# Weight slots skewed by 64 bytes each in a two-block transformer kernel, with the delta columns moved into a spent mask

## The chip, the cores and the metric

One NeuronCore of a Trainium2 chip runs the whole kernel. The metric is the device time in microseconds (us) of one execution: the median of three runs.

## The reference

Two transformer-like blocks follow each other on a sequence of 512 tokens with 1024 channels, all in float32. The first projects its input to queries, keys, values and gates, runs a matrix LSTM over chunks and a sparse attention, and merges both. The second has a feed-forward layer (hidden width 2816), a mixer with a gated delta rule and a pooling branch, and a second feed-forward layer. Nearly all the arithmetic is in products of activations with weights:

```python
h = modulate(rms_norm(x, norm_g[l, 0]), shift[:, 0], scale[:, 0])
x = x + 0.5 * gate[:, 0, None, :] * swiglu(h, ffn1_w_in[l], ffn1_w_out[l])
h = modulate(rms_norm(x, norm_g[l, 1]), shift[:, 1], scale[:, 1])
x = x + gate[:, 1, None, :] * token_mixer(h, mix_w_in[l], conv_w[l], ...)
```

## The kernel before

**Three matmuls for one.** A float32 product is made of three matmuls in the type F32R. Each operand is split into a high part (itself, rounded to F32R) and a low part (the rest). `mm3` (lines 432 to 436) issues high weight by high activation, high weight by low activation, and low weight by high activation, all into one PSUM bank. The weight block of 128 x 128 is the stationary operand, loaded before each of the three (LDWEIGHTS, the engine PEld of the profile); the activations, 512 tokens wide, are the moving operand. Only `v1` and `vsw1` (lines 988 to 990) have the two the other way round.

**Chunks and slots.** All weights pass through four slots in turn. SyncE loads a chunk of 128 x 1024 numbers into `w_raw` (`load_chunk`, line 399); ScalarE makes the high part (`split_hi`, line 385) and VectorE the low one (`split_lo`, line 393); TensorE uses the chunk as eight blocks of 128 columns (`pe_tile`) and marks it done, which lets ScalarE write the slot again. Chunk n has slot n % 4. The splits run two chunks ahead of TensorE (`AHEAD = 2`). The list `STAGES` sets the order of chunks: `v1`, `conv1`, `small1`, `nsa1` and so on to `ffn2_out`, 307 in all. `ffn1_in` and `ffn2_in` have 44 chunks each, with `act_hi` and `act_lo` as moving operand; `ffn1_out` and `ffn2_out` have 24 chunks of 8, 8 and 6 blocks with `ffn_hi` and `ffn_lo`. Each merge takes gates from `act`, one branch from `ya` (first block) or `pool` (second), the other from `yb`; the output projections take `merged`. In the stages between `vsw1` and `merge1`, and from `k2` to `z2`, other small matmuls in plain F32 are laid between blocks of the weight chunks by hand; `mods` puts sums for the modulation between chunks in the first stages (line 894).

**The layout.** Every buffer has a fixed byte offset in its partition's row. `fixed` (line 172) places buffers one after the other from byte 16512 on, each rounded up to 32 bytes; what follows the last of them, PH, is where `phase` places buffers that share memory over time, at a given number of KB from PH:

```python
XT = fixed("residual", [KD, T])
HHI, HLO = fixed("act_hi", [KD, T], F32R), fixed("act_lo", [KD, T], F32R)
RAW = fixed("w_raw", [4, 1024])
WHI, WLO = fixed("w_hi", [4, 1024], F32R), fixed("w_lo", [4, 1024], F32R)
CST = fixed("constants", [K_ALL])
PAR = fixed("params", [PAR_ALL])
```

`residual`, `act_hi`, `act_lo`, `w_raw`, `w_hi` and `w_lo` have 16384 bytes each; `constants` has 1729 columns (6944 bytes with rounding) and `params` 984 (3936 bytes). A row ends at byte 229344. The moving operands `ffn`, `merged`, `ya`, `yb` and `pool` are phase buffers; those of `act` are fixed ones.

**The delta columns.** `delta_cols` holds nine groups of 32 columns of small per-token factors of the delta rule (`dcol`, line 508). They are written from the stage `k2` on (line 2061 and lines 2759 to 2799) and read by VectorE, ScalarE and GpSimd, and by TensorE at lines 1342 and 1343. The causal mask, 512 columns of the constants from K_CM on, is read at line 2582 in the first block's attention.

Of the kernel before, what the change touches and what calls it, by code (L numbers as in the profile page):

```python
# [19 lines left out]
F32R = mybir.dt.float32r  # L20
# [32 lines left out]
K_ID, K_ONE, K_CM, K_CMT, K_ROPE, K_SWAP, K_LV = 0, 128, 256, 768, 896, 1024, 1152  # L53
# [104 lines left out]
def two_blocks(nc, cst, x, positions, norm_g, w_in, conv_q_w, conv_q_b, conv_k_w, conv_k_b, b_igate,  # L158
# [6 lines left out]
    with ctx:  # L165
# [6 lines left out]
        def fixed(name, shape, dt=F32):  # L172
            t = nc.alloc_sbuf_tensor_at(name, [P, *shape], dt, offset=at[0])
            at[0] += -(-int(np.prod(shape)) * 4 // 32) * 32
            return t
# [1 line left out]
        XT = fixed("residual", [KD, T])  # L177
        HHI, HLO = fixed("act_hi", [KD, T], F32R), fixed("act_lo", [KD, T], F32R)
        RAW = fixed("w_raw", [4, 1024])
        WHI, WLO = fixed("w_hi", [4, 1024], F32R), fixed("w_lo", [4, 1024], F32R)  # L180
        CST = fixed("constants", [K_ALL])
        PAR = fixed("params", [PAR_ALL])
        PH = at[0]
# [1 line left out]
        def phase(name, kb, shape, dt=F32):  # L185

            off = PH + int(kb * KB)
            assert off + int(np.prod(shape)) * 4 <= 229344, (name, off, shape)
            return nc.alloc_sbuf_tensor_at(name, [P, *shape], dt, offset=off)
# [61 lines left out]
        SS, KDT = phase("delta_state", 88, [DH, P]), phase("delta_k_dec", 92, [DH, P])  # L251
        SMR2 = phase("beta_rows", 92, [T])
        ML = phase("delta_level", 96, [DH, P])
        DC = phase("delta_cols", 100, [288])
        Y2HI, Y2LO = phase("yb2_hi", 48, [KD, T], F32R), phase("yb2_lo", 64, [KD, T], F32R)
        PLHI, PLLO = phase("pool_hi", 80, [4, T], F32R), phase("pool_lo", 40, [4, T], F32R)
        PLW = phase("pool_w", 88, [4, P])
# [14 lines left out]
        def sem(name):  # L272
            if name not in names:
                names[name] = ctx.enter_context(nc.semaphore(name))
            return names[name]

        w_loaded = [sem(f"w_loaded{k}") for k in range(4)]
        w_hi, w_lo, chunk_done = sem("w_hi_ready"), sem("w_lo_ready"), sem("chunk_done")
# [229 lines left out]
        def dcol(n, k=32):  # L508
            return DC[:, n:n + k]

# [2511 lines left out]
```

## Time and profile before

| | |
|---|---|
| device time, three runs | 1966.59, 1968.11, 1969.8 us |
| median | 1968.11 us |
| profiled execution, its span | 1970.5 us |
| mean granted TensorE clock | 0.995 |
| TensorE busy, weight loads busy | 98%, 81% |
| VectorE, ScalarE, GpSimd busy | 51%, 37%, 10% |
| data moved | 212.89 MB, mean 108 GB/s |

The span is that of the profiled execution, from its first instruction to its last; the profile gives no time around it. Engines are named PE (matmuls), PEld (weight loads), DVE (VectorE), ACT (ScalarE), POOL (GpSimd) and SP (SyncE). A matmul's duration is longer than the distance to the next one's start, since they overlap in the engine; the pace is read from the starts.

### The profile page before, as it was taken

The page shows a single profiled execution, that of the slowest core. Times are in us where ns is not written, and L with a number is a line of the kernel's source. Part 1 is how long each engine was busy: PE and PEld are TensorE (multiplying, and loading weights), DVE is VectorE, ACT ScalarE, POOL GpSimd, SP SyncE. Part 2 cuts the span into 40 slices and gives each one's busy share as a digit, 9 for nine tenths or more (in the row PEclk, how much of TensorE's full clock was granted, in tenths as well). Part 3 has the DMA queues.
Part 4 walks back from the last instruction along what each step waited for, and adds up shares of the span by engine and source line. Part 5 has one row for each costly group of instructions (what it writes and reads, how often), then busy time and mean ns, then how long its engine had stood idle before and what let it go on. Part 6 is the DMA issues. An engine that isn't in the chain of part 4 may idle for free.

```text
span 1970.5 us, 25809 instructions
## 1 busy us (share of the span) xinstructions
PE 1934.5 (98%) x9544; PEld 1588.1 (81%) x9544; DVE 1010.2 (51%) x1413; ACT 738.3 (37%) x1293; POOL 192.4 (10%) x242
## 2 busy tenths in 40 slices
PE   7999999999999999999999999999999999999998
PEld 5888878766688888888887788898888888888887
DVE  6787766575454563333334666445633573333332
ACT  4344333465533342223222664343522352222332
POOL 1101110000000000000011235035000000000010
PEclk9999999999999999999999999999999999999999
DMA  8967913311134323332333333210334323333331
GB/s 312 324 172 240 303 46 91 84 33 45 30 109 121 94 86 101 92 104 88 103 89 101 83 86 88 70 46 27 94 99 137 98 86 106 96 96 93 99 98 53
DMA packets 330903, 212.89 MB, mean 108 GB/s; under 512 B 21373, under 2 KB 315450, under 8 KB 330302
## 3 DMA queue, kind: packets, MB, share of 16 engines
q1 hardware_dynamic: 319830, 170.27, 30.0%
q0 software_dynamic: 10368, 37.75, 5.4%
q10 hardware_dynamic: 616, 3.67, 0.5%
q8 instruction: 58, 0.95, 0.2%
q14 instruction: 31, 0.25, 0.0%
HBM read 204.31 MB, written 7.35 MB: 107 GB/s over the span
## 4 chain that ended last, share of the span: by engine, by line
PE 93%; DVE 4%; ACT 1%; DMA 1%; issue 1%; ACTq 0%; POOL 0%; DVEq 0%; POOLq 0%
PE psum L434 26%; PE psum L436 25%; PE psum L435 25%; PE psum L1470 2%; PE psum L1256 1%; PE psum L1288 1%; PE psum L988 1%; PE psum L990 1%; PE psum L989 1%; PE psum L1269 1%; DVE ada_sum L2222 1%; DMA ada_w<-in_ada_w 1%; DVE delta_qkv_T L2222 1%; PE psum L1154 1%; PE psum L1170 1%
## 5 line engine op out<-in xcount | busy, mean ns | idle before, releaser
L434 PE MATMUL psum<-act_hi,w_hi 128*128 128x512 f32 x1616 | 648.5, 401 | 4.8 <-DVE act_lo L2222 2.5
L436 PE MATMUL psum<-act_hi,w_lo 128*128 128x512 f32 x1616 | 631.9, 391 | 0.0
L435 PE MATMUL psum<-act_lo,w_hi 128*128 128x512 f32 x1616 | 630.7, 390 | 0.0
L393 DVE TENSOR_TENSOR w_lo<-w_raw,w_hi 128x1024 fp32r<-128x1024 f32 x306 | 383.3, 1256 | 319.9 <-ACT w_hi L385 298.1
L385 ACT ACTIVATE w_hi<-w_raw 128x1024 fp32r<-128x1024 f32 x306 | 319.4, 1051 | 186.9 <-PE psum L436 179.0
L434 PEld LDWEIGHTS psum<-act_hi,w_hi 128*128 128x128 f32 x1616 | 304.2, 188 | 83.1 <-issue 19.5
L436 PEld LDWEIGHTS psum<-act_hi,w_lo 128*128 128x128 f32 x1616 | 303.9, 188 | 65.3
L435 PEld LDWEIGHTS psum<-act_lo,w_hi 128*128 128x128 f32 x1616 | 304.5, 188 | 61.3 <-issue 1.4
L764 POOL TENSOR_TENSOR squares<-squares 128x512 f32<-128x512 f32 x18 | 29.0, 1610 | 1249.9 <-ACT squares L1658 1249.9
L434 PE MATMUL psum<-ffn_hi,w_hi 128*128 128x512 f32 (+1 forms) x374 | 143.4, 384 | 0.0
L436 PE MATMUL psum<-ffn_hi,w_lo 128*128 128x512 f32 (+1 forms) x374 | 142.7, 382 | 0.0
L435 PE MATMUL psum<-ffn_lo,w_hi 128*128 128x512 f32 (+1 forms) x374 | 142.7, 381 | 0.0
L1751 ACT ACTIVATE ffn_hi<-ffn_tmp 128x512 f32 (+1 forms) x44 | 27.8, 632 | 206.9 <-DVEq L2717 206.9
L2222 DVE SCALAR_TENSOR_TENSOR ada_sum<-ada_w,params,ada_sum 128x1024 f32<-128x1024 f32 x63 | 80.8, 1282 | 16.3 <-DMA ada_w<-in_ada_w 14.2
L2222 DVE SCALAR_TENSOR_TENSOR residual<-psum,params,residual 128x512 f32<-128x512 f32 (+1 forms) x25 | 18.3, 730 | 130.2 <-PE psum L436 130.2
L2222 DVE SCALAR_TENSOR_TENSOR delta_qkv_T<-psum,params,delta_qkv_T 128x511 f32<-128x511 f32 (+3 forms) x96 | 60.3, 647 | 46.4 <-ACT delta_qkv_T L2047 44.7
L2219 DVE TENSOR_TENSOR ffn_tmp<-ffn_tmp,psum 128x512 f32<-128x512 f32 x42 | 28.9, 687 | 107.5 <-PE psum L436 107.5
L436 PEld LDWEIGHTS psum<-ffn_hi,w_lo 128*128 128x128 f32 x374 | 70.3, 188 | 14.9
L435 PEld LDWEIGHTS psum<-ffn_lo,w_hi 128*128 128x128 f32 x374 | 70.3, 188 | 14.7
L434 PEld LDWEIGHTS psum<-ffn_hi,w_hi 128*128 128x128 f32 x374 | 70.3, 188 | 14.6
L2018 ACT ACTIVATE ffn_tmp<-psum 128x512 f32<-128x512 f32 x42 | 25.1, 598 | 104.3 <-PE psum L436 104.3
L2219 DVE TENSOR_TENSOR ffn_lo<-ffn_tmp,ffn_hi 128x512 f32 (+1 forms) x44 | 30.5, 693 | 49.8 <-ACT ffn_hi L1751 49.8
(369 smaller groups left out, 2352.1 us busy)
## 6 DMA issues: line engine op xcount, KB each, us to landing
w_raw<-in_ffn_w_in SPq DMA_DIRECT2D x88, 512.0 KB, 3.8
ada_w<-in_ada_w POOLq DMA_DIRECT2D x72, 512.0 KB, 5.7
w_raw<-in_w_in SPq DMA_DIRECT2D x68, 512.0 KB, 4.1
w_raw<-in_mix_w_in SPq DMA_DIRECT2D x52, 512.0 KB, 3.9
w_raw<-in_ffn_w_out SPq DMA_DIRECT2D x32, 512.0 KB, 4.2
w_raw<-in_ffn_w_out SPq DMA_DIRECT2D x16, 384.0 KB, 3.4
w_raw<-in_w_branch_a SPq DMA_DIRECT2D x8, 512.0 KB, 4.1
w_raw<-in_w_out SPq DMA_DIRECT2D x8, 512.0 KB, 4.0
```

The source lines that it names most:

```text
L385: act.activation(WHI[:, n % 4, :], RAW[:, n % 4, :], ACT.Copy).then_inc(w_hi, 1)
L393: dve.tensor_tensor(WLO[:, n % 4, :], RAW[:, n % 4, :], WHI[:, n % 4, :].bitcast(F32), ALU.subtract).then_inc(w_lo, 1)
L434: pe.matmul(out, whi, hhi, start=start, stop=False)
L435: pe.matmul(out, whi, hlo, start=False, stop=False)
L436: return pe.matmul(out, wlo, hhi, start=False, stop=stop)
L764: pool.tensor_tensor(SQ[:, 0, :], SQ[:, 0, :], SQ[:, square_slot(r, k), :], ALU.add)\
L988: pe.matmul(o, HHI[:, kt, tok], WHI[:, n % 4, w], start=(kt == 0), stop=False)
L1470: mm = pe.matmul(PS[:, bank, (h % 4) * P:(h % 4) * P + P], left(h), right(h), start=True, stop=True)
L1751: act.activation(dst, src, ACT.Copy).then_inc(u_hi, 1)
L2018: act.activation(FS[:, f, :], PS[:, pl.bank(2 * f), :], ACT.Silu)\
L2219: return dve.tensor_tensor(o, a, b, op)
L2222: return dve.scalar_tensor_tensor(o, a, s, b, op0, op1)
```

## The change

The two tensors `w_hi` and `w_lo` become one, `w_split`, of four slots. A slot is 2 x 1024 + 16 columns: the high part, the low part, and 16 columns (64 bytes) that nothing uses. `WHI` and `WLO` are slices of it, and every use stays as it is written. `delta_cols` loses its phase buffer and becomes a view of the first 288 columns of the causal mask.

```diff
         RAW = fixed("w_raw", [4, 1024])
-        WHI, WLO = fixed("w_hi", [4, 1024], F32R), fixed("w_lo", [4, 1024], F32R)
+        WSPLIT = fixed("w_split", [4, 2 * 1024 + 16], F32R)
+        WHI, WLO = WSPLIT[:, :, 0:1024], WSPLIT[:, :, 1024:2048]
         CST = fixed("constants", [K_ALL])
...
         ML = phase("delta_level", 96, [DH, P])
-        DC = phase("delta_cols", 100, [288])
+        DC = CST[:, K_CM:K_CM + 288]
```

## Rows read from the trace of the kernel before

**Rows 1.** The page: busy time, share of the span, instructions of each engine.

```profile
PE 1934.5 (98%) x9544; PEld 1588.1 (81%) x9544; DVE 1010.2 (51%) x1413; ACT 738.3 (37%) x1293; POOL 192.4 (10%) x242
```

**Rows 2.** The page: the chain that ended last, by engine and by line.

```profile
PE 93%; DVE 4%; ACT 1%; DMA 1%; issue 1%; ACTq 0%; POOL 0%; DVEq 0%; POOLq 0%
PE psum L434 26%; PE psum L436 25%; PE psum L435 25%; PE psum L1470 2%; PE psum L1256 1%; PE psum L1288 1%; PE psum L988 1%; PE psum L990 1%; PE psum L989 1%; PE psum L1269 1%; DVE ada_sum L2222 1%; DMA ada_w<-in_ada_w 1%; DVE delta_qkv_T L2222 1%; PE psum L1154 1%; PE psum L1170 1%
```

**Rows 3.** Who waited for whom: us in total, times, longest us.

```profile
DVE w_lo L393 <- ACT w_hi L385: 298.1, 117, 6.9
...
PEld psum L988 <- DVE w_lo L393: 1.2, 1, 1.2
```

**Rows 4.** Instructions by line and shape: busy us, mean ns, idle before.

```profile
L434 PE MATMUL psum<-act_hi,w_hi 128*128 128x512 f32 x1616 | 648.5, 401 | 4.8 <-DVE act_lo L2222 2.5 <-DVEq L2396 1.8 <-ACT nsa_v_tokens L1584 0.5
...
L393 DVE TENSOR_TENSOR w_lo<-w_raw,w_hi 128x1024 fp32r<-128x1024 f32 x306 | 383.3, 1256 | 319.9 <-ACT w_hi L385 298.1 <-DVE delta_qkv_T L2222 5.6 <-DVE mlstm_qk_T L2222 4.5
L385 ACT ACTIVATE w_hi<-w_raw 128x1024 fp32r<-128x1024 f32 x306 | 319.4, 1051 | 186.9 <-PE psum L436 179.0 <-PE psum L990 3.5 <-DMA w_raw<-in_mix_w_in 3.2
...
L434 PE MATMUL psum<-ffn_hi,w_hi 128*128 128x512 f32 x330 | 130.8, 396 | 0.0
```

**Rows 5.** Timeline of TensorE in `ffn1_in`, then `ffn1_out`: start us, duration us.

```profile
899.71 0.39 PE L434 MATMUL psum<-act_hi,w_hi 128*128 128x512 f32 x1
...
901.75 0.39 PE L434 MATMUL psum<-act_hi,w_hi 128*128 128x512 f32 x1
...
999.77 0.40 PE L436 MATMUL psum<-ffn_hi,w_lo 128*128 128x512 f32 x1
...
1002.34 0.39 PE L435 MATMUL psum<-ffn_lo,w_hi 128*128 128x512 f32 x1
```

**Rows 6.** TensorE by stretch: length, busy us (count), clock, DMA share, GB/s.

```profile
739.00:939.00 200.00, 200.00 (x884) 1.00 0.33 96
...
1010.00:1060.00 50.00, 50.00 (x216) 1.00 0.31 82
...
962.28:966.48 4.20, 4.20 (x20) 1.00 0.59 175
...
1649.72:1655.16 5.44, 5.44 (x26) 1.00 0.23 69
...
1666.04:1671.48 5.44, 5.44 (x26) 1.00 0.43 125
```

**Rows 7.** Timeline of TensorE in `merge1`, a `ya` tile, then `yb` (28 starts).

```profile
556.92 0.40 PE L434 MATMUL psum<-ya_hi,w_hi 128*128 128x512 f32 x1
...
563.22 0.39 PE L434 MATMUL psum<-yb_hi,w_hi 128*128 128x512 f32 x1
```

**Rows 8.** Timeline of weight loads in `ffn1_in`, for the load at 900.17.

```profile
900.17 0.19 PEld L434 LDWEIGHTS psum<-act_hi,w_hi 128*128 128x128 f32 x1
```

**Rows 9.** Timeline of TensorE after the modulation sums interrupted `nsa1`.

```profile
208.81 0.39 PE L435 MATMUL psum<-act_lo,w_hi 128*128 128x512 f32 x1
209.04 0.40 PE L436 MATMUL psum<-act_hi,w_lo 128*128 128x512 f32 x1
209.28 0.40 PE L434 MATMUL psum<-act_hi,w_hi 128*128 128x512 f32 x1
...
210.90 0.39 PE L435 MATMUL psum<-act_lo,w_hi 128*128 128x512 f32 x1
211.12 0.39 PE L436 MATMUL psum<-act_hi,w_lo 128*128 128x512 f32 x1
...
213.39 0.39 PE L434 MATMUL psum<-act_hi,w_hi 128*128 128x512 f32 x1
```

**Rows 10.** Timeline of TensorE: six F32 records of 257 columns, and the next.

```profile
302.92 1.47 PE L1170 MATMUL psum<-mlstm_v_tokens,mlstm_decay_probs 128*128 128x257 f32 x6
304.22 0.50 PE L1154 MATMUL psum<-mlstm_qk_T 128*128 128x128 f32 x3
```

**Rows 11.** Line 1342: duration ns min/median/max, first and last start.

```profile
L1342 PE MATMUL psum<-delta_cols,constants x2: 276/286/297, 1109.6 to 1109.7; 128*128 128x32 f32 x2
```

## The prediction

> **What bounds the kernel now.** I read the page's shares first: TensorE is busy for 98% of the span and no other engine for more than 51% [rows 1]. The chain that ended last says the same: 93% of it is TensorE, and three lines of one helper, `mm3`, make up 76% [rows 2]. So only what alters the pace of those matmuls, or makes them wait, can move the time.
>
> Then the waits. on the split of a weight (`w_lo`) the weight load waits once, for 1.2 us, while VectorE stands 298 us behind ScalarE in making it [rows 3]. The weights are ready well ahead.
>
> Then the pace itself, which is what this change can touch. A matmul's own duration (390 to 401 ns [rows 4]) doesn't give it, because matmuls overlap: the distance between two starts does. In `ffn1_in`, ten starts lie 2.04 us apart from first to last, 0.2267 us each. In `ffn1_out`, twelve starts are 2.57 us apart, 0.2336 us each [rows 5]. Both are 128x128 by 128x512, same engine, same helper, same weight slots, granted clock 1.00 in both [rows 6]. Two long windows give the same: 884 matmuls in 200 us, less the one or two cut by the edges, is 226.8 ns; 216 in 50 us is 233 ns [rows 6]. Chunk by chunk it is 5.44 us for 24 matmuls, in slot 0 as in slot 3 three chunks later (the two between are alike), and 4.20 us for the 18 of a short chunk in `ffn1_out` [rows 6]. So there are two steady levels, **226.7 ns and 233.3 ns**, and the slot's number has no part in either.
>
> What differs between the two is where the moving operand lies. The layout is arithmetic on the code: `w_hi` starts at byte 16512 + 65536 = 82048 of its row, which is 128 past a multiple of 256, and `w_lo` and every slot and every 128-column block keep that. `act_hi` (32896) and `act_lo` (49280) are also 128 past a multiple. PH, where the phase buffers begin, is 125696, a multiple of 256, and so is every phase buffer, all at quarters of a KB. `ya` and `yb` go at the same 0.233 us as `ffn`, although `yb_lo` (56.25 KB) lies 256 bytes otherwise within 512 than the rest [rows 7]. So steps of 256 bytes don't matter, one of 128 does. I read it as the weight load, which begins with the running matmul (900.17 us is the third start of the first stretch) [rows 5, 8], and the moving operand meeting in the memory: distance 0 (modulo 256) costs 226.7, distance 128 costs 233.3.
>
> There is a third thing. After other work has broken the stream, activation matmuls take about ten starts to fall into step: 208.81 to 211.12 us is ten starts in 2.31 us, 231 ns each, with the same addresses, and the next ten, to 213.39, take 2.27 us, 227 ns each [rows 9]. So 226.7 is a state that the stream locks into, not the cost of any one matmul.
>
> **The change, part by part.**
> *The skew.* A slot of the new tensor is 2064 columns, 8256 bytes: slot 1 lies 64 bytes, slot 2 128 and slot 3 192 further modulo 256; `w_lo` is 4096 further than `w_hi`, which changes nothing modulo 256. The tensor is 256 bytes longer than the two it replaces, so constants, parameters and all phase buffers move by 256: nothing. By instructions nothing is added or taken away. New distances, weights from moving operand: activations 0, 64, 128, 192 for slots 0 to 3; phase operands 128, 192, 0, 64.
>
> *Counts.* Activations as moving operand or weights: 3 x 1616 by `mm3` [rows 4] and 192 in `v1`, 5040. Phase operands, 512 wide: `ffn` 330 by the rows [rows 4], and by the code's loops merged 128, `yb` 96, `ya` 64, pool 32, so 3 x 650 = 1950. Of the 210 activation chunks 121 run unbroken (33 up to `nsa1`, 44 in each `ffn_in`), 2904 matmuls; of the other 2136 about half are locked, by the ten starts of [rows 9] out of 24. So some 3900 are at 226.7, about 975 a slot; phase operands about 488 a slot.
>
> *Slot 0*: nothing changes, 0 us.
> *Slot 2*: both levels are known, and swap. Activations 975 x (+6.67 ns) = +6.5 us; phase operands 488 x (-6.67) = -3.3 us.
> *Slots 1 and 3*: no row has a distance of 64 or 192. Bounds: from below, a stream without any meeting. An F32 record of 257 columns, which streams at half the pace, takes 1.30 / 6 = 0.217 us [rows 10], so 0.843 ns a column and at the full pace 216 ns for 512. From above, two starts in the unlocked stretch stand 0.24 us apart [rows 9]. I take the middle of the two locked levels, 230 ns, since a stream with these lengths passes through all distances anyway and each known level is one of just two; the unlocked mean of 231 is near it too. Activations 1950 x (+3.33) = +6.5 us; phase operands 975 x (-3.33) = -3.2 us.
> *Changes of distance at each chunk's border*: today the stream changes distance only between stages, and a transient of the kind in [rows 9] follows. With some 300 borders and a few ns each, +1 us; between -1 and +5.
> *Sum*: 6.5 - 3.3 + 6.5 - 3.2 + 1 = **+7.5 us**.
>
> *The split's own work.* ScalarE's 1051 ns and VectorE's 1256 ns for a slot [rows 4] may shift with the new addresses. A tenth on the latter is 306 x 0.126 = 39 us of VectorE, hidden: the weight load waited 1.2 us on it in all [rows 3]. 0 us; without the cover it would be some of those 39.
> *DMA.* `w_raw` stays where it was, each load waits on the same count of splits. 0 us.
> *The delta columns.* They move into 288 columns of the causal mask, which VectorE reads last in the first block's attention (line 2582), long before `k2` writes the first sum there. They had to leave: 100 KB + 1152 bytes past the new PH is beyond the end of the row. The same operations start again on a multiple of 64 bytes; no wait is added and nothing is queued behind one. TensorE reads them in four short records (32 columns, 276 to 297 ns [rows 11]). 0 us.
>
> Against the profiled execution, whose span is 1970.5 us, the sum gives 1978.0; that span is 2.4 above the median of the three runs, so against the median 1968.1 it gives **1975.6 us**.
>
> **Where a rule would have it otherwise.** The rows show two levels by address alone [rows 5, 6]. The Trainium skill, "TensorE: Matmul & The Clock Gate", section "Step-by-step: what each phase is for", says that the moving operand and the weight load have read ports of their own, so that loading the next weights takes no read bandwidth from the running matmul. By that rule no shift of a weight could change the pace and the sum would be 0; the trace speaks against it with 226.7 and 233.3 ns for equal work, but not for certain, as the next part says.
>
> **The rivals.**
> *A, no change, 1968.1 us (what the rule just named gives too).* The level may go by the moving operand's own address and not by its distance from the weights. In the trace of before the weights never move modulo 256, so no row tells the two apart; and the moving operands keep theirs after the change, so nothing would happen. Against it: an address alone has nothing to meet, and F32 records reading the same regions lose almost nothing [rows 10].
> *B, faster, about 1955 us.* Distances 64 and 192 avoid the meeting. Fully, at 216 ns: activations 1950 x (-10.7) = -21 us, the unlocked ones of those slots 570 x (-15) = -9, phase operands 975 x (-17.3) = -17, with slot 2 and the borders +4: -43 us, 1925. At 222 ns it is about -9 - 5 - 11 + 4 = -21, and if one of the two distances gains and the other doesn't, about -13: 1955. The point from which it decides: 1950(p - 226.7) + 975(p - 233.3) = -4.2 us, p = 227.5 ns for the mean of the two slots. For it: nothing excludes it. Against it: the unlocked stretch drifts through many alignments and no start in it comes sooner than 0.22 us after the last [rows 9].
> *C, slower still, 1987 us.* Skewed slots never lock. At 232 ns activations give 1950 x 5.3 = +10 us, phase operands -1, slot 2 and borders +5: 1982; at 236 ns +18 +3 +5 = 1994. For it: locking is special to distance 0 and takes ten starts of 24, and here each chunk changes the distance.
>
> **How the numbers follow.** Forecast (one or both odd slots between the levels, 1970 to 1981): 0.34. A: 0.17. B: 0.32. C: 0.17. A measurement of this kernel tells 0.2%, some 4 us, from no change. Slower by more: forecast and C less a little, 0.49; same: A and the edges, 0.19; faster: 0.32. The range holds 8 in 10 by running from B's half (a gain of 20 us) to C's upper part: 1947 to 1991. The forecast's own range is 1970 to 1981; cases of both signs have weight.
>
> **What would show it.** Right: in `ffn1_in` chunks of slot 0 stay at 5.44 us for 24, slot 2 shows 5.60, slots 1 and 3 something between; in `ffn1_out` slot 0 stays at 5.60 and slot 2 drops to 5.44. The number of matmuls in 200 us falls from 884 to about 871. Wrong: all four slots at 5.44 (A), odd slots below 5.44 (B), all but slot 0 at 5.57 or more (C); or TensorE waiting on `w_lo` for more than a few us.

## The result

The changed kernel takes 1982.2 us (median of 8 runs, 1978.8 to 1986.2), the kernel before 1969.4 us in the same set (8 runs, 1966.6 to 1975.5). The ratio is **1.0056** (95% interval 1.0041 to 1.0070): slower by 0.56%, about 11 us. The two medians alone stand 12.9 us apart, which the interval still holds; the ratio is taken as the measure. Forecast were +7.5 us and a range of 1947 to 1991; the sign and the mechanism held, the odd slots were priced too low.

The page of the profile after: span, busy time, and the chain that ended last. TensorE carries the span as in [rows 1, 2]; it is busy 13.4 us longer and the span is 14.0 us longer.

```profile
span 1984.5 us, 25809 instructions
...
PE 1947.9 (98%) x9544; PEld 1593.2 (80%) x9544; DVE 1010.2 (51%) x1413; ACT 738.1 (37%) x1293; POOL 192.1 (10%) x242
...
PE 92%; DVE 3%; DMA 2%; ACT 1%; issue 1%; ACTq 0%; POOL 0%; SPq 0%; DVEq 0%; POOLq 0%
PE psum L435 26%; PE psum L437 25%; PE psum L436 25%; PE psum L1471 2%; PE psum L1257 1%; PE psum L1289 1%; PE psum L989 1%; PE psum L990 1%; PE psum L991 1%; DMA ada_w<-in_ada_w 1%; PE psum L1270 1%; DVE ada_sum L2223 1%; DVE delta_qkv_T L2223 1%; PE psum L1155 1%; PE psum L1171 1%
```

Groups by line and shape (one line later than before, since the diff adds a line), and the wait of the low part's split for the high part's. ScalarE's and VectorE's work on a slot takes 1051 and 1253 ns, where [rows 4] have 1051 and 1256, and the wait is 303.1 us where [rows 3] had 298.1. The splits are not what became slower.

```profile
L394 DVE TENSOR_TENSOR w_split<-w_raw,w_split 128x1024 fp32r<-128x1024 f32 x306 | 382.6, 1253 | 325.0 <-ACT w_split L386 303.1 <-DVE delta_qkv_T L2223 5.7 <-DVE mlstm_qk_T L2223 4.5
L386 ACT ACTIVATE w_split<-w_raw 128x1024 fp32r<-128x1024 f32 x306 | 319.3, 1051 | 186.9 <-PE psum L437 179.0 <-PE psum L991 3.6 <-DMA w_raw<-in_mix_w_in 3.1
```

```profile
DVE w_split L394 <- ACT w_split L386: 303.1, 117, 6.9
```

TensorE in the same two stretches of 200 us in the feed-forward layers: length, busy us (count), clock. 869 matmuls where [rows 6] had 884, at clock 1.00 and with no idle time: each start comes some 230.5 ns after the last (22.13 us for 96 starts in the next rows), not 226.7.

```profile
739.00:939.00 200.00, 200.00 (x869) 1.00 0.33 95
1634.00:1834.00 200.00, 200.00 (x869) 1.00 0.34 98
```

Then chunk by chunk. The timeline of TensorE in `ffn1_in` of the kernel after, the first matmul of five chunks, slots 0, 1, 2, 3 and 0; 24 starts lie from one row to the next.

```profile
755.22 0.39 PE L435 MATMUL psum<-act_hi,w_split 128*128 128x512 f32 x1
...
760.67 0.40 PE L435 MATMUL psum<-act_hi,w_split 128*128 128x512 f32 x1
...
766.27 0.39 PE L435 MATMUL psum<-act_hi,w_split 128*128 128x512 f32 x1
...
771.84 0.39 PE L435 MATMUL psum<-act_hi,w_split 128*128 128x512 f32 x1
...
777.35 0.39 PE L435 MATMUL psum<-act_hi,w_split 128*128 128x512 f32 x1
```

The differences are 5.45, 5.60, 5.57 and 5.51 us for slots 0 to 3, and they repeat to 0.01 us over the last 40 chunks of each `ffn_in`, which run unbroken. The same in `ffn1_out`: slots 2, 3, 0, 1 and 2, where the chunk of slot 3 (second row) has 18 matmuls.

```profile
984.95 0.39 PE L435 MATMUL psum<-ffn_hi,w_split 128*128 128x512 f32 x1
...
990.39 0.40 PE L435 MATMUL psum<-ffn_hi,w_split 128*128 128x512 f32 x1
...
994.59 0.39 PE L435 MATMUL psum<-ffn_hi,w_split 128*128 128x512 f32 x1
...
1000.16 0.39 PE L435 MATMUL psum<-ffn_hi,w_split 128*128 128x512 f32 x1
...
1005.68 0.39 PE L435 MATMUL psum<-ffn_hi,w_split 128*128 128x512 f32 x1
```

Slot 2 takes 5.44 us, slot 3 4.20 (5.60 for 24), slot 0 5.57, slot 1 5.51. Every buffer has its old place modulo 256 except the weights of slots 1 to 3, and the two lists are the same four numbers in another order. Put by distance (weights from moving operand, modulo 256) they agree: 0 gives 5.44 to 5.45, 64 gives 5.60, 128 gives 5.57, 192 gives 5.51.

In `v1` the roles are swapped: the activations are loaded and the weights stream, so the distance of slot 1 is -64, which is 192. The first matmuls of slots 1, 2 and 3 in `v1`:

```profile
27.33 0.40 PE L989 MATMUL psum<-w_split,act_hi 128*128 128x512 f32 x1
...
32.84 0.40 PE L989 MATMUL psum<-w_split,act_hi 128*128 128x512 f32 x1
...
38.43 0.40 PE L989 MATMUL psum<-w_split,act_hi 128*128 128x512 f32 x1
```

Slot 1 takes 5.51 us, the price of 192, where in `ffn1_in` the same slot at 64 takes 5.60; slot 2, at 128 both ways, takes 5.59. That is one chunk; experiment e5 below repeats it. There the weights of all slots lie 64 bytes beyond the activations, `ffn1_in` takes 5.60 us a chunk, and the two unbroken chunks of `v1`, by the same counting at 192, take 10.99 us together, 5.50 each:

```profile
26.70 0.39 PE L990 MATMUL psum<-w_split,act_hi 128*128 128x512 f32 x1
...
37.69 0.39 PE L990 MATMUL psum<-w_split,act_hi 128*128 128x512 f32 x1
```

So the distance counts from the operand that is loaded to the one that streams, and it doesn't matter which of them is a weight.

Where the 14.0 us of the trace went, from the first start of each stage's first chunk to that of the next: `v1` +0.6, `conv1` +1.4, `small1` and `nsa1` +1.9, `vsw1` to `ga1` +1.4, `ffn1_in` +4.1, `small2` +0.4, `k2` to `z2` +2.0, `merge2` +1.2, `ffn2_in` +4.1 us; and on phase operands `out1` -0.4, `ffn1_out` -0.6, `out2` -0.5, `ffn2_out` -1.1. `merge1` stays, and what lies ahead of `v1` is 0.7 shorter. The 24 chunks of `ffn1_out` themselves gain 1.5; what stands between its last chunk and `small2` takes 0.9 longer, for a reason given further on (*The rest*). The activations lose, the phase operands gain less, as the forecast had it.

### The profile page after: what moved, and what is told of

Read it like the earlier page. It is cut to its first block, busy times and chain, and to the rows that moved or that the text cites. A ratio compares the mean times of both kernels' runs of the same rounds, so it can differ in the third digit from the quotient of the medians.

```text
span 1984.5 us, 25809 instructions
## 1 busy us (share of the span) xinstructions
PE 1947.9 (98%) x9544; PEld 1593.2 (80%) x9544; DVE 1010.2 (51%) x1413; ACT 738.1 (37%) x1293; POOL 192.1 (10%) x242
## 4 chain that ended last, share of the span: by engine, by line
PE 92%; DVE 3%; DMA 2%; ACT 1%; issue 1%; ACTq 0%; POOL 0%; SPq 0%; DVEq 0%; POOLq 0%
PE psum L435 26%; PE psum L437 25%; PE psum L436 25%; PE psum L1471 2%; PE psum L1257 1%; PE psum L1289 1%; PE psum L989 1%; PE psum L990 1%; PE psum L991 1%; DMA ada_w<-in_ada_w 1%; PE psum L1270 1%; DVE ada_sum L2223 1%; DVE delta_qkv_T L2223 1%; PE psum L1155 1%; PE psum L1171 1%
## 5 line engine op out<-in xcount | busy, mean ns | idle before, releaser
L435 PE MATMUL psum<-act_hi,w_split 128*128 128x512 f32 x1616 | 653.8, 405 | 4.8 <-DVE act_lo L2223 2.5
L437 PE MATMUL psum<-act_hi,w_split 128*128 128x512 f32 x1616 | 637.0, 394 | 0.0
L436 PE MATMUL psum<-act_lo,w_split 128*128 128x512 f32 x1616 | 636.0, 394 | 0.0
L394 DVE TENSOR_TENSOR w_split<-w_raw,w_split 128x1024 fp32r<-128x1024 f32 x306 | 382.6, 1253 | 325.0 <-ACT w_split L386 303.1
L386 ACT ACTIVATE w_split<-w_raw 128x1024 fp32r<-128x1024 f32 x306 | 319.3, 1051 | 186.9 <-PE psum L437 179.0
L435 PEld LDWEIGHTS psum<-act_hi,w_split 128*128 128x128 f32 x1616 | 305.2, 189 | 87.0 <-issue 19.6
L437 PEld LDWEIGHTS psum<-act_hi,w_split 128*128 128x128 f32 x1616 | 304.6, 188 | 69.5
L436 PEld LDWEIGHTS psum<-act_lo,w_split 128*128 128x128 f32 x1616 | 305.0, 189 | 65.4 <-issue 1.4
L435 PE MATMUL psum<-ffn_hi,w_split 128*128 128x512 f32 (+1 forms) x374 | 142.8, 382 | 0.0
L437 PE MATMUL psum<-ffn_hi,w_split 128*128 128x512 f32 (+1 forms) x374 | 142.1, 380 | 0.0
L436 PE MATMUL psum<-ffn_lo,w_split 128*128 128x512 f32 (+1 forms) x374 | 142.0, 380 | 0.0
L437 PEld LDWEIGHTS psum<-ffn_hi,w_split 128*128 128x128 f32 x374 | 70.4, 188 | 14.1
L436 PEld LDWEIGHTS psum<-ffn_lo,w_split 128*128 128x128 f32 x374 | 70.4, 188 | 13.8
L435 PEld LDWEIGHTS psum<-ffn_hi,w_split 128*128 128x128 f32 x374 | 70.5, 188 | 13.7
```

The lines of the kernel that those rows point to most:

```text
L386: act.activation(WHI[:, n % 4, :], RAW[:, n % 4, :], ACT.Copy).then_inc(w_hi, 1)
L394: dve.tensor_tensor(WLO[:, n % 4, :], RAW[:, n % 4, :], WHI[:, n % 4, :].bitcast(F32), ALU.subtract).then_inc(w_lo, 1)
L435: pe.matmul(out, whi, hhi, start=start, stop=False)
L436: pe.matmul(out, whi, hlo, start=False, stop=False)
L437: return pe.matmul(out, wlo, hhi, start=False, stop=stop)
```

## The experiments

**e1: no skew.** The 16 spare columns go; all else of the change stays.

```diff
-        WSPLIT = fixed("w_split", [4, 2 * 1024 + 16], F32R)
+        WSPLIT = fixed("w_split", [4, 2 * 1024], F32R)
```

> The changed kernel without the 16 spare columns: high and low parts of a slot still lie side by side, the delta columns still lie in the mask, but every slot starts at the same place modulo 256 as in the kernel before, and the phase buffers too. Theory 1 (the pace goes by the distance modulo 256 between the weight block being loaded and the moving operand): as the kernel before, within 0.2% of 1969 us; 5.44 us for 24 matmuls in every slot of ffn1_in, 5.60 in ffn1_out. Theory 2 (the side-by-side layout or the delta columns cost something by themselves): it stays near 1982 us, or part of the way.

1970.8 us against 1972.6 us before on the same chip, ratio 0.9995 (0.9982 to 1.0007): no difference. The first matmuls of two chunks of `ffn1_in` four apart, then of two neighbours in `ffn1_out`:

```profile
747.30 0.39 PE L435 MATMUL psum<-act_hi,w_split 128*128 128x512 f32 x1
...
769.07 0.39 PE L435 MATMUL psum<-act_hi,w_split 128*128 128x512 f32 x1
...
968.50 0.40 PE L435 MATMUL psum<-ffn_hi,w_split 128*128 128x512 f32 x1
...
974.10 0.40 PE L435 MATMUL psum<-ffn_hi,w_split 128*128 128x512 f32 x1
```

21.76 us for four chunks, 5.44 each, and 5.60 us for the next pair, as before. So the side-by-side layout and the delta columns in the mask cost nothing that shows, both together; theory 2 falls. The whole loss is the skew's. The two weren't tried apart, since together they come to nothing.

**e2: phase buffers 128 bytes later.** As e1, with one line more.

```diff
+        at[0] += 128
         PH = at[0]
```

> As e1, and all phase buffers start 128 bytes later, so that ffn, merged, ya, yb and pool too lie at distance 0 modulo 256 from the weights. Theory 1: ffn1_out goes at 5.44 us for 24 instead of 5.60; 1950 matmuls save 6.3 to 6.7 ns each, 12 to 13 us, so about 1956 us. Theory 3 (the weights' own address sets the pace, the moving operand's has no part): no change against e1, 1969 us, 5.60 us for 24 in ffn1_out.

1957.6 us against 1972.6, ratio **0.9927** (0.9912 to 0.9941), 14 us faster than the kernel before. The timeline in `ffn1_out`, the first matmuls of chunks in slots 1, 2, 3 (18 matmuls), 0 and 1:

```profile
962.60 0.39 PE L436 MATMUL psum<-ffn_hi,w_split 128*128 128x512 f32 x1
...
968.04 0.39 PE L436 MATMUL psum<-ffn_hi,w_split 128*128 128x512 f32 x1
...
973.48 0.39 PE L436 MATMUL psum<-ffn_hi,w_split 128*128 128x512 f32 x1
...
977.56 0.39 PE L436 MATMUL psum<-ffn_hi,w_split 128*128 128x512 f32 x1
...
983.00 0.39 PE L436 MATMUL psum<-ffn_hi,w_split 128*128 128x512 f32 x1
```

5.44, 5.44, 4.08 and 5.44 us: the phase operands now go like the activations. The weights weren't moved modulo 256, so theory 3, the weights' own address, falls; and the kernel after, which moves the weights and not the moving operands, had already ruled out the moving operand's own address (rival A of the forecast). Stages on phase operands give up 11.8 us of the trace (`merge1` 1.9, `out1` 0.8, `ffn1_out` 3.5, `merge2` 1.9, `out2` 1.3, `ffn2_out` 2.4), just under the 12 to 13 expected. The other 5.2 us of the trace aren't the distance's: 4.6 of them lie in `nsa1`, `vsw1` and `ga1`. At the end of `nsa1` TensorE doesn't wait for the modulation sums in this trace, where before it did, and each of the other two has a stretch at a lower granted clock before (0.83 over 222 to 232 us, 0.84 over 445 to 456) and none here (1.00 in both; see *The rest*). This version beats both kernels. It needs the delta columns out of the end of the row: with them at 100 KB the row would be 32 bytes too short.

**e3 and e4: all distances in steps of 16 bytes.** The skew is 4 columns instead of 16; e4 also starts the weights 128 bytes later and the phase buffers another 128.

```diff
-        WSPLIT = fixed("w_split", [4, 2 * 1024 + 16], F32R)
+        at[0] += 128                                          # e4 only
+        WSPLIT = fixed("w_split", [4, 2 * 1024 + 4], F32R)
...
+        at[0] += 128                                          # e4 only
         PH = at[0]
```

> Skew of 16 bytes a slot instead of 64: distances of 0, 16, 32 and 48 in ffn1_in and 64, 80, 96 and 112 in ffn1_out (slots 0 to 3). The changed kernel gave, for 24 matmuls, 5.45 us at 0, 5.60 at 64, 5.57 at 128 and 5.51 at 192. Theory 1: each slot has a time of its own between 5.4 and 5.65 us, 5.60 again at 64 although it is now slot 0 of a phase buffer, and a smooth rise from 0 to 64. Theory 4 (only multiples of 64 count, as memory lines): slots 0 to 3 of ffn1_in all at 5.44 us and of ffn1_out all at 5.60. Time: 1975 to 1985 by theory 1, about 1969 to 1971 by theory 4.

> The other half of the circle: skew of 16 bytes a slot, weights 128 bytes later and phase buffers moved to fit: distances of 128, 144, 160 and 176 in ffn1_in and 192, 208, 224 and 240 in ffn1_out. Theory 1: about 5.57 at 128 (slot 0 of ffn1_in), 5.51 at 192 (slot 0 of ffn1_out), and a fall towards 5.44 at 240, which lies next to 0; time 1978 to 1990 us, since all activations leave distance 0. Theory 4: all slots of ffn1_in at 5.57, of ffn1_out at 5.51.

One run each, where runs of the kernel before spread over 10 us: e3 1984.1 us, e4 1986.1 us. First matmuls of chunks in e3, in `ffn1_in` (slots 0, 1, 2, 3, 0), at distances 0, 16, 32 and 48:

```profile
751.44 0.40 PE L435 MATMUL psum<-act_hi,w_split 128*128 128x512 f32 x1
...
756.90 0.39 PE L435 MATMUL psum<-act_hi,w_split 128*128 128x512 f32 x1
...
762.35 0.39 PE L435 MATMUL psum<-act_hi,w_split 128*128 128x512 f32 x1
...
767.94 0.40 PE L435 MATMUL psum<-act_hi,w_split 128*128 128x512 f32 x1
...
773.54 0.40 PE L435 MATMUL psum<-act_hi,w_split 128*128 128x512 f32 x1
```

In e4, in `ffn1_out` (slots 3, 0, 1, 2, 3; the chunk of slot 0 has 18 matmuls), at distances 240, 192, 208 and 224:

```profile
1030.09 0.40 PE L437 MATMUL psum<-ffn_hi,w_split 128*128 128x512 f32 x1
...
1035.55 0.39 PE L437 MATMUL psum<-ffn_hi,w_split 128*128 128x512 f32 x1
...
1039.67 0.40 PE L437 MATMUL psum<-ffn_hi,w_split 128*128 128x512 f32 x1
...
1045.24 0.39 PE L437 MATMUL psum<-ffn_hi,w_split 128*128 128x512 f32 x1
...
1050.83 0.40 PE L437 MATMUL psum<-ffn_hi,w_split 128*128 128x512 f32 x1
```

The other half of the distances is read in the same way in `ffn1_out` of e3 and `ffn1_in` of e4. For 24 matmuls this gives (18 scaled up, the chunk's entry included; at 0, 64, 128 and 192 the kernel after agrees):

| distance | 0 | 16 | 32 | 48 | 64 | 80 | 96 | 112 |
|---|---|---|---|---|---|---|---|---|
| us | 5.46 | 5.45 | 5.59 | 5.60 | 5.60 | 5.56 | 5.62 | 5.60 |

| distance | 128 | 144 | 160 | 176 | 192 | 208 | 224 | 240 |
|---|---|---|---|---|---|---|---|---|
| us | 5.57 | 5.60 | 5.60 | 5.52 | 5.51 | 5.57 | 5.60 | 5.46 |

Three of 16 distances, 240, 0 and 16, are near 5.45 (240 unsteadily: its chunks in `ffn1_out` take between 5.44 and 5.51, and the one unbroken chunk of `v1` in e3 that lies at 240 takes 5.56). Two, 176 and 192, are at 5.5, and all others at 5.56 to 5.62. Outside of 0, 64, 128 and 192 each distance has been seen with one kind of moving operand in the main, and always after a chunk at a neighbouring distance, so the last digit is that of this order of chunks. Theory 4 falls, for 16 bytes decide between 5.45 and 5.59. Theory 1's smooth rise from 0 to 64 falls too: it is a step between 16 and 32. And no distance is below 5.44, so none of these skews could have gained on the activations, which sat at the best place already.

**e5: one distance for all.** As e1, with all weights 64 bytes later, and the phase buffers with them, so that their distance stays 128.

```diff
+        at[0] += 64
         WSPLIT = fixed("w_split", [4, 2 * 1024], F32R)
```

> As e1 (no skew), but all four slots start 64 bytes later, and so do the phase buffers: activations at distance 64 in every slot, phase operands at 128 as in the kernel before. No distance changes from one chunk to the next. Theory 1, with the distance itself as the cause: 5.60 us for 24 matmuls in all slots of ffn1_in, 5.60 in ffn1_out; 3900 locked matmuls lose 6.7 ns, 26 us, so about 1995 us, worse than the changed kernel although nothing is skewed. Theory 5 (the loss of the change comes from changing the distance at every chunk, not from the distances): all slots fall into step again at about 5.44, about 1970 us.

1994.7 us against 1968.8, ratio 1.0122 (1.0105 to 1.0139), 24 us slower. Two chunks of `ffn1_in` four apart, and TensorE in the stretch of 200 us:

```profile
755.62 0.39 PE L436 MATMUL psum<-act_hi,w_split 128*128 128x512 f32 x1
...
778.02 0.39 PE L436 MATMUL psum<-act_hi,w_split 128*128 128x512 f32 x1
```

```profile
739.00:939.00 200.00, 200.00 (x858) 1.00 0.31 92
```

22.40 us for four chunks is 5.60 each, 858 matmuls in 200 us where before had 884. The distance itself is the cost; a change of distance at each chunk isn't needed for it, and theory 5 falls. The skewed kernel is cheaper than this one only because its other slots lie at better distances.

**e6: one of the two moving operands off.** As e1, with `act_lo` 128 bytes on.

```diff
-        HHI, HLO = fixed("act_hi", [KD, T], F32R), fixed("act_lo", [KD, T], F32R)
+        HHI = fixed("act_hi", [KD, T], F32R)
+        at[0] += 128
+        HLO = fixed("act_lo", [KD, T], F32R)
+        at[0] += 128
```

> As e1, but act_lo alone starts 128 bytes later than act_hi modulo 256: of three matmuls on activations two stream act_hi at distance 0 and one act_lo at distance 128, with the same weights. Theory 1 with a cost of each matmul by itself: two at 226.7 and one at about 232 to 233.3, so 5.49 us for 24, about +8 us in all. Theory 1 with the step of the whole stream as the thing that counts: a third of the matmuls off is enough to lose it, every matmul at about 231 to 233, 5.55 to 5.60 us for 24, +20 to +26 us, 1989 to 1995 us. Theory 3 (weights' own address): 5.44 us, 1969 us.

1989.3 us, ratio 1.0094 (1.0076 to 1.0111), 19 us slower. Two chunks of `ffn1_in` four apart:

```profile
756.19 0.40 PE L438 MATMUL psum<-act_hi,w_split 128*128 128x512 f32 x1
...
778.59 0.40 PE L438 MATMUL psum<-act_hi,w_split 128*128 128x512 f32 x1
```

Again 22.40 us, 5.60 a chunk, though two of three matmuls stream at distance 0. In `ffn2_in`, with the same addresses, a chunk takes 5.55 us: the stream has settled into another pattern there. So the cost isn't paid matmul by matmul at its own distance, which would have given 5.49; the stream as a whole is in step or out of it, and one matmul in three is enough to put it out. One rival stands: the shift also parts `act_lo` from `act_hi`, which stream one after the other. A run with `w_lo`, which is loaded while `act_lo` streams, shifted with it would tell the two apart; there is none.

## Why the prediction was right

*The bound, the waits, the splits, the delta columns, the move by 256.* All as forecast; no weight load of the kernel after waits for a split, and e1 shows the delta columns and the side-by-side layout to be nothing within 0.2%.

*Two levels by distance.* Right. It rested on phase buffers and activations alone, with the rival that the moving operand's own address decides; the four distances of the kernel after and e2 settle it.

*Slot 0.* Forecast 0 on activations; its chunks take 5.45 instead of 5.44 us, since after slot 3 the stream needs some four starts to fall into step. That is 0.5 ns a matmul, within the +1 us for the borders. On phase operands it was to stay at 5.60 and takes 5.574 at the same distance of 128, which gives the half microsecond back.

*Slot 2.* Forecast +6.7 ns on activations, measured (5.574 - 5.440) / 24 = +5.6; forecast -6.7 on phase operands, measured (5.447 - 5.600) / 24 = -6.4. The same distance of 128 gives 5.60 where the stream never leaves it and 5.57 where it comes from another: two patterns at one distance, which the forecast didn't have.

*Slots 1 and 3: the term that was mis-sized.* The middle, 230 ns for each, was taken. Measured are 5.60 / 24 = 233.3 at distance 64 and 5.51 / 24 = 229.6 at 192, mean 231.4. On activations that is 1950 x 4.75 = +9.3 us where +6.5 stood. Phase operands got 233.3 in slot 3, where the merges give them 606 of 1950 matmuls, and 229.6 in slot 1, with 396: -1.5 us where -3.2 stood. With slot 2 at +5.5 and -3.3 the sum becomes about +10 us, and the ratio says +11.

*What of it was luck.* The middle for the odd slots rested on no row at their distances, and slot 1 isn't between the levels but at the upper one (5.60), against what was to show the forecast right. By the forecast's own chances slower stood against faster as 0.49 to 0.32, and the range reached from a gain of 21 us to a loss of 23, so that the time fell inside it says little. The median, 1982.2, is also the figure that C had for 232 ns, and the measured mean of the odd slots, 231.4, is nearer to C's than to the forecast's 230. What the runs bear out is the two levels by distance, slot 2 in both directions, and the zeros.

*The rest.* The trace has 14.0 us, 3 more than the ratio. The two profiled executions differ in the granted clock. TensorE around the start of `vsw1` and around `small2`, before and after, and then e1 for the first of the two; the figure after the count is the granted clock:

```profile
222.00:232.00 10.00, 10.00 (x73) 0.83 0.94 328
...
1066.00:1086.00 20.00, 16.01 (x67) 0.83 0.44 145
...
222.00:232.00 10.00, 8.58 (x47) 0.66 0.98 307
...
1066.00:1086.00 20.00, 15.24 (x63) 0.74 0.37 131
...
222.00:232.00 10.00, 10.00 (x86) 1.00 0.98 364
```

The clock has two levels, 2.4 GHz (1.00) and 1.2 GHz (0.50), so 0.83 in the first stretch is a third of it at the lower one, and 0.66 two thirds; e1, with the same work, has nothing of it there. Ahead of it TensorE waits for the modulation sums and runs 16 matmuls of one column on them. It stood idle for 1.72 us there in the trace of after and for 1.16 before, and the clock fell; for 0.88 in e1 and not at all in e2, and it didn't. In the trace of after that break takes 1.2 us more than before, part idle time and part the lower clock. `vsw1` is 0.8 us longer, `small2` 0.4, and the end of `ffn1_out` 0.9: there eight matmuls, on `rms_diagonal`, take 2.08 us where they took 1.16. That is 3.3 us, and leaves 10.7. The times of all runs say the same. Of the kernel before and e1, on one chip, five runs at a mean granted clock of 0.993 took 1974.2 to 1976.2 us and six at 0.995 took 1968.4 to 1972.3; the kernel after took 1986.2 at 0.993, which is the profiled run, and 1980.1 to 1981.5 at 0.995. At equal clocks the two kernels are 10 to 12 us apart.

*The stages with interleaved work.* `k2` to `z2` lose 2.0 us of the trace. Half of their 36 chunks at the mean loss of 0.093 us would be 1.7, so the forecast's "about half are locked" was near enough there.

*Two flaws in the reading.* The chunk windows of [rows 6] were set by hand and don't begin on chunk borders. The rates in them hold, the slot numbers given with them don't; e1 above, whose starts do lie on borders, shows what they were meant to show. And 2904 matmuls and half of 2136 are some 3970 locked ones, not 3900, which moves the sum by less than 0.2 us.

*The rivals.* A (no change) fell with the kernel after. B (odd slots faster than 227.5 ns on average) had the largest chance beside the forecast, 0.32, and the map shows it had no ground: none of 16 distances gives less than 226.7 with 512 columns. What spoke against it in the trace, that no start after an interruption came sooner than 0.22 us, was worth more than it was given. C (never in step) is half true: distances 64 and 128 aren't locked at 226.7, but each settles into a steady pattern of its own, it doesn't drift. Nor were its signs all there: slot 3 takes 5.51, under the 5.57 that C asks for.

*The rule on separate read ports.* The Trainium skill, "TensorE: Matmul & The Clock Gate", section "Step-by-step: what each phase is for", has it that loading the next weights takes nothing from the running matmul. By the runs, moving the loaded operand by 64 bytes against the streaming one costs 24 us here (e5), and aligning the two saves 14 (e2). The measurement decides: for F32R matmuls with 512 moving columns and a weight load each, the pace depends on how the loaded operand lies to the streaming one. Whether it is the two reads that meet, or something else that goes by both addresses, no run tells apart.

## What to carry to other kernels

Where TensorE runs F32R matmuls of 512 columns back to back with a weight load each, read the distance between starts, not the durations, and compare stages of equal shape: 3% between them (5.44 and 5.60 us) was nothing but the buffers' byte offsets here. Put the operand that is loaded and the one that streams at the same place modulo 256 bytes, for all operands of the stream, and keep slots a multiple of 256 apart (with 256 columns the order of the distances is another, as the last section shows); a skew that looks like spreading the accesses can take the stream off the best place. Compare executions at equal granted clocks before a difference of a few microseconds is put down to the change. Before a layout change, ask which distance each stage has now: here most of the work was already at the best one and the smaller part at a poor one, so shifting that part was the gain to be had.

## What the runs showed of the hardware

- The pace of F32R matmuls with 512 columns depends on the distance, modulo 256 bytes, from the loaded to the streaming operand: 226.7 ns at 0, 227.0 at 16, between the levels and unsteady at 240, 229 to 234 elsewhere, worst at 96 (5.62 us for 24, 234 ns). Steps of 256 bytes don't matter (`yb_lo` in [rows 7]; constants, parameters and phase buffers after the change).
- The stream has a memory. At one distance it can be in several steady patterns (at 128, 233.3 ns or 232.3), and it takes some four starts after a change of distance and some ten after other work to reach 226.7.
- Even in step, at distance 0, a matmul costs 13.3 ns more than its columns. In e1, the first matmul of `vsw1`'s second chunk, with 256 columns, and the 24th after it:

```profile
227.54 0.28 PE L989 MATMUL psum<-w_split,act_hi 128*128 128x256 f32 x1
...
230.42 0.28 PE L989 MATMUL psum<-w_split,act_hi 128*128 128x256 f32 x1
```

0.120 us each against 0.2267 with 512 columns: 256 columns more take 106.7 ns, which is 2.4 columns a ns, and 13.3 ns remain in both. The Trainium skill, "TensorE: Matmul & The Clock Gate", section "Back-to-back issue gap", gives 2.5 ns over the columns for a matmul by itself, and about 131 ns for one of 512 columns in a stream with weight loads. Neither holds for the F32R stream here: it has 13.3 ns over the columns, and 226.7 ns is its best at 512 columns. Whether it is the weight load of each matmul that costs the 13.3 ns wasn't tried, since no form of the kernel here streams without one.
- With 256 columns the order of the distances turns round. The same two places of `vsw1`'s second chunk in e3, where the distance is 224, worth 5.60 us with 512 columns:

```profile
229.24 0.28 PE L989 MATMUL psum<-w_split,act_hi 128*128 128x256 f32 x1
...
232.04 0.28 PE L989 MATMUL psum<-w_split,act_hi 128*128 128x256 f32 x1
```

2.80 us for 24, 116.7 ns each, faster than the 120.0 at distance 0. This chunk takes 118.5 ns a matmul in the kernel after (distance 128), 117.8 in e5 (192) and 118.8 in e4 (96). So 0 is the best place with 512 columns and the slowest of those seen with 256, and the 13.3 ns are the price of that step, not a least cost of every matmul.
- At the lower clock the 13.3 ns don't show. Before the change, `vsw1` begins in the stretch at 1.2 GHz, with the same 256 columns at distance 0:

```profile
223.71 0.41 PE L989 MATMUL psum<-w_lo,act_hi 128*128 128x256 f32 x1
...
226.06 0.30 PE L988 MATMUL psum<-w_hi,act_hi 128*128 128x256 f32 x1
```

Eleven starts take 2.35 us, 213.6 ns each, and 256 columns at 1.2 a ns are 213.3.

No run showed what it is that goes by the two addresses, or why its period is 256 bytes.
